# A two-layer hybrid encoder in one kernel: a table built in two halves two steps apart, and a projection's half products joined in the attention steps without value products

## The reference, cut to what matters

```
proj = h @ w_in                       # 1024 x (3*8*64 + 3*8*64)
# mixer A: three dilated windows, merged by their softmax denominators,
#          T5 bias by relative position
# mixer B: tokens on a grid 64 wide (16 rows); a query sees 8 rows x 16 columns
s = einsum('brqhd,brkwhd->bhrqkw', q, k) * D**-0.5
s = where(col_ok, s + rpb[h, row offset, column offset], -1e30)
o = softmax(s) @ v
```

## Time and profile before

| | us |
|---|---|
| median of 3 runs | 2953.62 (2951.68 to 2955.04) |
| the profiled execution, its own time | 2948.45 |
| its span, first to last instruction | 2946.6 |
| TensorE matmuls busy | 2732.3 (93%) |
| TensorE weight loads busy | 2257.8 (77%) |
| VectorE busy | 1742.1 (59%) |
| ScalarE busy | 949.6 (32%) |
| GpSimd busy | 1419.4 (48%) |
| mean granted TensorE clock | 0.972 of full speed |

### The profile page before, as it was taken

One profiled execution on the slowest core, in us unless ns is written; L12 is line 12 of the kernel. 1 busy time (PEld: TensorE's weight loads), 2 busy tenths in 40 slices (PEclk: granted clock), 3 DMA queues, 4 the chain that ended last, 5 costly groups with the idle time before them and its releaser, 6 DMA issues. The chain is left out here.

```text
span 2946.6 us, 41486 instructions
## 1 busy us (share of the span) xinstructions
PE 2732.3 (93%) x13508; PEld 2257.8 (77%) x13508; DVE 1742.1 (59%) x2827; ACT 949.6 (32%) x1754; POOL 1419.4 (48%) x1334
## 2 busy tenths in 40 slices
PE   6899999987999999999984999999799999999996
PEld 4788887766877887887763888888677887888874
DVE  5565655553756555565545777777638555455555
ACT  3555544451411100011123666667514100011001
POOL 2333334445656655666621433333466655566554
PEclk9999999998999999999997999999899999999998
DMA  4433334324311111111214334433333111111111
GB/s 140 116 97 87 83 77 98 80 79 147 98 57 43 57 50 46 57 46 57 71 53 93 90 95 100 109 90 92 128 103 86 55 52 43 53 53 55 52 43 71
DMA packets 271430, 228.53 MB, mean 78 GB/s; under 512 B 44345, under 2 KB 237233, under 8 KB 270609
## 3 DMA queue, kind: packets, MB, share of 16 engines
q1 hardware_dynamic: 269639, 212.89, 26.5%
q10 hardware_dynamic: 1667, 14.07, 1.2%
HBM read 158.22 MB, written 17.04 MB: 59 GB/s over the span
## 5 line engine op out<-in xcount | busy, mean ns | idle before, releaser
L693 POOL TENSOR_SCALAR xT<-xT,rden 128x1024 f32<-128x1024 f32 (+2 forms) x256 | 281.7, 1101 | 707.4 <-DVE rden L1675 707.4
L718 POOL TENSOR_TENSOR ring<-block_t,ring 128x512 fp32r<-128x512 f32 x320 | 420.8, 1315 | 25.5
L1683 DVE TENSOR_TENSOR pt<-psD,pt 128x512 fp32r<-128x512 f32 (+2 forms) x512 | 303.4, 634 | 156.6 <-ACT pt L1275 156.3
L1031 PE MATMUL psS<-times_r,ring 128*128 128x512 f32 x928 | 366.2, 395 | 16.1 <-ACT rstd L1385 9.4
L716 POOL CAST ring<-block_t 128x512 fp32r<-128x512 f32 x320 | 213.6, 668 | 340.9 <-PE psD L1065 138.3
L1032 PE MATMUL psS<-times_r,ring 128*128 128x512 f32 x928 | 362.6, 391 | 0.0
L1033 PE MATMUL psS<-times_r,ring 128*128 128x512 f32 x928 | 362.2, 390 | 0.0
L1844 DVE TENSOR_TENSOR xT<-psD,xT 128x512 f32<-128x512 f32 x352 | 240.4, 690 | 201.6 <-PE psD L1065 201.6
L1275 ACT ACTIVATE pt<-psD 128x512 fp32r<-128x512 f32 (+2 forms) x512 | 258.3, 557 | 189.5 <-PE psD L881 188.5
L1063 PE MATMUL psD<-act,ring 128*128 128x512 f32 x704 | 279.5, 397 | 14.0 <-DVE act L1816 6.7
L1667 DVE CUSTOM_DVE_ANT_0 xT<-psS,xT 128x1024 f32<-128x1024 f32 (+2 forms) x256 | 287.6, 1123 | 3.5 <-PE psS L868 2.7
(11 more groups left out here) (214 smaller groups left out, 4888.3 us busy)
## 6 DMA issues: line engine op xcount, KB each, us to landing
block_t<-in_w_gate SPq DMA_DIRECT2D x96, 256.0 KB, 2.9
block_t<-in_w_up SPq DMA_DIRECT2D x96, 256.0 KB, 3.2
block_t<-in_w_down SPq DMA_DIRECT2D x88, 256.0 KB, 3.1
kq<-split_x SPq DMA_DIRECT2D x130, 128.0 KB, 2.4
kq<-row SPq DMA_DIRECT2D x126, 128.0 KB, 2.3
xT<-rel_c SPq DMA_DIRECT2D x16, 960.0 KB, 5.6
stage<-in_w_even SPq DMA_DIRECT2D x24, 512.0 KB, 4.1
heads<-o_out SPq DMA_DIRECT2D x128, 64.0 KB, 2.1
```

What stands on the lines that cost most here:

```text
L693: pool.tensor_scalar(s, s, rden[:, t % 4:t % 4 + 1], 1.0, ALU.mult, ALU.mult).then_inc(S["normed"], 1)
L718: pool.tensor_tensor(lo, src, hi.bitcast(F32), ALU.subtract).then_inc(S["ws"], 1)
L1031: pe.matmul(o, unit(u, 0)[:, w], hi, start=first and k == 0, stop=False)
L1683: ve.tensor_tensor(PT[:, 1, j0:j1, t % 3, :], blocks(psT[b][:, 0:(j1 - j0) * P]), PT[:, 0, j0:j1, t % 3, :].bitcast(F32), ALU.subtract).th ...
```

## The change

`filler_even` gives work only in the steps 5, 7, ... 15 (x even), and the tensor program then issues both halves of the product one after the other. As `filler_even` gives the part 1 with it, what follows a finished product (ScalarE's and VectorE's copies, SP's moves, each in the step behind) is one step earlier too. `build_b` gets a part: the columns' half in step 9 (heads 2p+2) or 5 (heads 2p+1), the other half in step 11 or 7. The first offsets of a pair are read in step 7 and not 5.

```diff
 def filler_even(t):
     pair, x = (t - 5) // NSTEP + 1, (t - 5) % NSTEP
-    if t >= 5 and pair < PAIRS and x < 12:
-        return pair, x // 2, x % 2
+    if t >= 5 and pair < PAIRS and x < 12 and x % 2 == 0:
+        return pair, x // 2, 1
     return None
@@ SP
-                if step == 5 and 3 <= pair < 7:
+                if step == 7 and 3 <= pair < 7:
                     offsets(2 * (pair - 3))
@@ TensorE
                 if filler_even(t):
-                    even_product(*filler_even(t))
+                    for part in range(2):
+                        even_product(*filler_even(t)[0:2], part)
@@ VectorE
-            def build_b(h):
-
-                ve.wait_ge(S["mask_in"], 16)
-                ve.wait_ge(S["offs_in"], 32 * (h - QB + 1))
+            def build_b(h, part):
+
                 rows = "p (r c) -> p r c"
                 off = xT[:, OFF_B:OFF_B + NROW * GRID]
-                col = rstd[:, 0:GRID].unsqueeze(1).broadcast_to([P, NROW, GRID])
-                ve.tensor_tensor(table(h)[:, 0:NROW * GRID].rearrange(rows, c=GRID),
-                                 off.rearrange(rows, c=GRID), col, ALU.add).then_inc(S["b_tab"], 1)
-                ve.tensor_tensor(table(h)[:, NROW * GRID:2 * NROW * GRID], off,
-                                 rstd[:, GRID:(NROW + 1) * GRID], ALU.add).then_inc(S["b_tab"], 1)
-                ve.wait_ge(S["b_tab"], 2 * (h - QB + 1))
+                if part == 0:
+                    ve.wait_ge(S["mask_in"], 16)
+                    ve.wait_ge(S["offs_in"], 32 * (h - QB + 1))
+                    col = rstd[:, 0:GRID].unsqueeze(1).broadcast_to([P, NROW, GRID])
+                    ve.tensor_tensor(table(h)[:, 0:NROW * GRID].rearrange(rows, c=GRID),
+                                     off.rearrange(rows, c=GRID), col, ALU.add).then_inc(S["b_tab"], 1)
+                else:
+                    ve.tensor_tensor(table(h)[:, NROW * GRID:2 * NROW * GRID], off,
+                                     rstd[:, GRID:(NROW + 1) * GRID], ALU.add).then_inc(S["b_tab"], 1)
+                    ve.wait_ge(S["b_tab"], 2 * (h - QB + 1))
...
-                if step == 10 and 3 <= pair < PAIRS - 1:
-                    build_b(2 * pair + 2)
-                if step == 3 and 4 <= pair < PAIRS:
-                    build_b(2 * pair + 1)
+                if step in (9, 11) and 3 <= pair < PAIRS - 1:
+                    build_b(2 * pair + 2, step // 11)
+                if step in (5, 7) and 4 <= pair < PAIRS:
+                    build_b(2 * pair + 1, step // 7)
```

## The result

The changed kernel takes 2930.22 us, the median of six runs (2927.43 to 2933.73), against 2951.65 for the kernel before in the same runs (2948.21 to 2955.04). The ratio is 0.9929 with a 95% interval of 0.9917 to 0.9942, that is 17 to 24.5 us less. Forecast were 2938.2 us and a range from 2932 to 2948.

The account below looks back on a forecast made before the run. TensorE was taken to set the pace where steps hold projection work, VectorE's order at two places. Terms 7.3 + 0.6 - 0.5 + 6.5 + 1.5 = 15.4 us gave 2933.0 from the profiled execution, 2938.2 us from the median; range 2932 to 2948.

Parts of the forecast that it names:

- the two named places: Where VectorE's order sets the pace: step 4 of pairs 4 to 7, and steps 7, 9, 11, 13 of pairs 4 to 6.
- The eviction's stall: Steps 7, 9, 11, 13 of pairs 4 to 6: 12 waits of 0.61 us gone, 0.5 us lost in short even steps.
- In pairs 0 to 3 ... nothing there: Joined products in pairs 0 to 3: no gain, as transposes and scores of 2 us already cover the eviction.
- The five light steps: Steps 0 to 4, without projection work: sixth product's copy moves from before step 1 into step 0, 3 x 0.2 = 0.6 us gained.
- The table: Step 4 of pairs 4 to 7: 6.5 us gained; 2.2 us of half tables in pair 7 swallowed by a wait.
- The clock: Pair 4's step 5: no fall to 1.2 GHz after the shortened wait, 1.5 us gained.
- the same difference from the median: Base: profiled execution 5.2 us below the median 2953.62; the same distance kept turns 2933.0 into 2938.2 us.
- (a): Step 4's gain mostly lost, transposes held by another chain (bias, exponent, copy): 4 x 0.5 instead of 6.5, 2944 us; chance 0.12.
- (d): Products still wait, on weights or on moves ahead of them; 6.5 + 1.5 remain, 2945 us; chance 0.04.
- (b): Short even steps run at ScalarE's and VectorE's pace in series, near 3.9 us: 2974 us, partly near 2960; chance 0.06.
- (c): Longer run of light steps lets the clock fall in every pair, 1.53 us each: 3.2 us gained, 2950 us; chance 0.08.
- (e): Later stretches with clock falls, from 646 us on, stand otherwise in time: gain up to 20 us, 2933 us; chance 0.08.

Follow-up runs that it names:

- e2: Kernel before with only the table changed (halves in steps 5 and 7, 9 and 11; offsets read in step 7): 2941.09 us, ratio 0.9968.
- e3: Kernel before with only the half products joined in odd steps, tables whole and placed as before: 2940.63 us, ratio 0.9972.
- e6: Changed kernel with the table in one piece, called in step 9 and step 5: 2931.78 us, ratio 0.9932.
- e4: Changed kernel with SP reading the heads of pair 7 earlier, in steps 1, 3 and 6: 2925.06 us, ratio 0.9919.
- e9: Kernel before, unedited, in a second profiled execution: 2947.53 us.
- e10: Kernel before, unedited, in a third profiled execution: 2953.80 us.
- e1: Changed kernel run again without edit: 2931.64 us, ratio 0.9938.
- e5: Changed kernel with whole products in the even steps, those with value products, in place of the odd ones: 2969.17 us, ratio 1.0062.
- e7: Kernel before with the table's second addition done twice: 2964.5 us, ratio 1.0046.
- e8: Changed kernel with earlier head reads, plus the output projection's first two weight blocks loaded in step 10 of the last pair: 2909.23 us, ratio 0.9857.

## Why the prediction was wrong

- **What bounds the kernel:** right. TensorE's steps set the time, and the two named places held all that was to be had, apart from the joins in A pairs. e2 and e3 show each without the other.
- **The eviction's stall, 12 x 0.61 - 0.5 = 6.8 us:** the mechanism is right, the term too small. The four steps with their even partners gave 2.6 to 2.7 us in each of three pairs, 8.0 in all, 1.2 more than the term. Nothing was lost in the short even steps, which keep the length of the subtraction (2.56, 2.33, 2.09, 2.31 us); and a joined product takes 0.05 us less than its two halves.
- **"In pairs 0 to 3 ... nothing there":** wrong by 1.1 us. There was no stall to remove, but two steps take 10.96 us instead of 11.02, at each of the joins. No row that I had of the kernel before shows it, and why a product in one piece is shorter stays open.
- **The five light steps, 0.6 us:** 0.65, right, and from pairs 5 to 7 with 0.2 us each, as worked out.
- **The table, 6.5 us:** 6.6 in the change, 6.6 in e2, right to 0.1; and hidden where it went, by e6 with room for a whole table. In pair 7 the half tables cost 1.3 us of the 2.2 feared (0.9 against the execution before, whose step 6 was 0.6 us slow itself), swallowed by the wait on the reads, as forecast. In e4, where most of that wait is gone, the steps keep this length.
- **The clock, 1.5 us:** right for the profiled execution, though the working overlooked that pair 7 had a fall of 0.6 us behind its step 4 as well. As a term it was read from one execution; e9 and e10 show 2.7 and 1.5.
- **The sum:** 15.4 against 17.0 measured between the profiled executions (17.2 to step 11 of pair 7, 17.6 without the 0.4 us at the beginning). The missing 2 us are the two terms above: 1.2 and 1.1.
- **The steps that failed:** two; without either of them the time would lie inside the range. First, two terms of the sum were too small: the eviction's stall, "12 x 0.61 = 7.3" less 0.5, gave 8.0, and the joins of pairs 0 to 3, put at nothing, gave 1.1. With these 2.3 us the forecast and its range move to 2935.9 and 2929.7 to 2945.7, which holds the time. Second, the base: "the same difference from the median gives 2938.2". It was the median of three runs, 2953.62, 5.2 us over the profiled execution; the same kernel has 2951.65 in six runs, 2949.44 in eighteen and 2951.40 in nine. I treated the 5.2 us as a fixed distance; they are scatter of single executions, 3.2 us of it visible at the start alone in e10. The changed kernel's medians, 2930.22 and 2931.64, lie 1.2 and 1.3 us below the profiled executions of their sets. The range had bounds for the change's costs but none for its own base; put on the profiled execution, 2933.0, the same range would reach from 2926.8 to 2942.8 and hold the time. From the eighteen runs, 2949.44 less 15.4 is 2934.0, and e1's 2931.64 lies 2.4 us below that: the two terms.
- **The rivals:** (a) and (d) are out (e2, e3). (b), the engines' pace in short steps, is real as a mechanism and is what e5 shows, 17.8 us slower than before; in the change the value products are the cover, and the even steps are 2.1 to 2.6 us long, not near 3.9. (c) is out: in neither profiled execution of the changed kernel did the clock fall in pairs 1 to 6 (granted clock 1.00 from 160 to 595 us in both). (e), more from later stretches, isn't supported: from pair 7's end to the end of the span the executions differ by 0.2 us.

What stays open: whether the gain between medians is 18 us or 21. Two sets of runs gave 18.3 and 21.0, with intervals that overlap; the falls of the clock behind the old step 4 cost 1.9 us on average over three executions, 0.4 more than the profiled pair shows, and don't explain 3.

## What to carry to other kernels

Price a moved piece of work by what stands behind it in the next step, not by its own length: the same join gains 8 us (e3) or loses some 28 (e5 against e2), depending on whether the step behind the product is long enough for the evictions. Take work off an in-order engine just ahead of an instruction that the bounding engine waits for; where it lands in a step with cover, even all of it in one piece costs nothing, up to an edge that should be computed (2.2 us were covered in step 10, 3.7 were not). And a forecast's base needs its own scatter in the range: three runs of a kernel whose executions differ by 10 us do not fix it to 2 us.

## What the runs showed of the hardware

VectorE and GpSimd hold each other up in both directions, and in these traces it is the instruction that starts second that is longer. I had expected only POOL's normalisation to suffer beside the additions. It does: 0.91 us for 768 columns when alone, 1.75 when it starts 0.6 us into one of the slowed additions of the changed kernel, 2.61 to 2.66 when it starts 0.2 us into the first of two, while those additions keep 1.08 or 1.09 (1.23 where the end of a split still runs). But VectorE's addition is slower when GpSimd's split of weights, with two inputs in SBUF, is already running. The first half table of pair 5 in the changed kernel, and that split:

```profile
483.52 1.61 DVE L1721 TENSOR_TENSOR xT<-xT,rstd 128x896 f32<-128x896 f32 x1
```
```profile
482.88 1.29 POOL L659 TENSOR_TENSOR W<-stage,W 128x512 fp32r<-128x512 f32 x1
```

1.6 us against 1.09 without that neighbour, while the split takes 1.29, as it does elsewhere (1.26 to 1.31); six of the sixteen additions of the changed kernel took 1.60 to 1.68 us. It cost nothing, as those steps last 6.6 us. The order decides, not the kind of operation: once, in e3, a normalisation started 0.17 us ahead of an addition, and there the normalisation kept its 0.90 us and the addition took 1.67:

```profile
578.92 1.67 DVE L1720 TENSOR_TENSOR xT<-xT,rstd 128x896 f32<-128x896 f32 x1 [0.27 <-issue]
```
```profile
578.75 0.90 POOL L693 TENSOR_SCALAR xT<-xT,rden 128x768 f32<-128x768 f32 x1 [3.99 <-DVE rden L1676]
```

The third additions of e7, in pairs 4 to 7, took 1.59 to 1.61 us behind a normalisation that had some 0.66 us left. In these rows the addition is longer by a little less than the time for which the earlier instruction still runs. That the later one waits until the earlier one has ended fits this; it is argued from the times, and no run was made to test it.

The granted clock fell to 1.2 GHz behind a wait of 2.1 to 2.25 us of TensorE in step 4, amid steps without projection work: in one or two of four such places, pairs 4 and 7 in the first execution of the kernel before, 4 and 6 in e9, 5 in e10, 5 and 7 in e3. Behind waits of 3.75 to 3.9 us it fell in all four (e7), behind waits of 0.5 us in the same surroundings never (the change, e1, e2, e4, e5, e6 and e8).
